# Layer attention with late scaling of its outputs, and norms split straight from PSUM

## The chip, the cores and the metric

The program runs on one core of one Trainium2 chip. The metric is the device time of one execution in microseconds (us). Two transformer blocks run one after the other in one launch.

## What is computed

The first block (attention over 8 grouped and 8 neighbourhood heads, a Fourier mix, a convolution, 16 experts) is followed by two layers of the second block; the change lies mostly in the layers.

```python
def hybrid_layer(x, ...):
    h = rms_norm_2(x, attn_norm_w)
    proj = h @ w_in
    mixed = concatenate([retention_mixer(...),   # 4 heads
                         dsa_mixer(...),         # 4 heads
                         dilated_mixer(...)])    # 8 heads
    x = x + mixed @ w_out
    h = rms_norm_2(x, mlp_norm_w)
    return x + jnp.square(jax.nn.relu(h @ w_up)) @ w_down

# dsa_mixer, per head, over the selected keys
p = jax.nn.softmax(jnp.where(valid, s, -jnp.inf), axis=-1)
return jnp.einsum('bhqn,bqnhd->bqhd', p, v_sel)
```

There are 512 tokens of width 1024, heads of 64 columns, and everything is float32. The three dilated branches come down to one softmax whose scores have the logarithm of a count added, so the 4 selected heads and the 8 dilated heads are the same computation, causal, with a different additive mask: 12 heads of "mixed attention" per layer.

## The kernel before

Every engine has one hand-written stream of instructions; semaphores tie them together (`T.next` works out the count to wait for), and loops are hardware loops. The order on each engine is the order in which the code is written.

Matrix products run as three float32r products of a rounded part and a remainder (`WH` and `WL` of a weight, `hH` and `hL` of an activation). A rounded part is made by ScalarE (ACT), the remainder by VectorE (DVE).

**Attention** (`attend` on TensorE (PE), ACT and DVE; `heads` on SyncE (SP), which issues the loads) works on tiles n of 128 query rows; a head has four (tt = 0 to 3), a pair of heads eight, and even and odd heads use buffers s = 0 and s = 1. In the layers tile tt sees (tt + 1) x 128 keys. For a tile, PE makes the scores (L816, L818); DVE adds the mask and takes the row's largest value in one instruction (L1838), then turns it into the exponential's bias (`NM`, L1752); ACT takes the exponential and sums it into `DEN` (L1278); DVE takes the reciprocal (L1759) and scales the probabilities with it (L1760); PE turns them (L828); ACT copies them out of PSUM (L1297). When a head's four tiles are there, PE multiplies with the values (L840) into `OT[s]`, 64 rows of bank 0. DVE then puts the head out (`put`, `to_split`, L2271 and L2272: the rounded part, then the remainder, each 64x512). In tile 1 of every head ACT rounds the next head's q and k (`rounded`, L1271, L1272), and DVE makes the remainders (`remainders`, L1737, L1738), after which PE may start that head's scores. DVE runs one tile ahead: in step n it issues

```python
top((n + 1) % (2 * NT), ...)
normalise(n)
...
if tt == 1:
    if not (last and s == 1):
        remainders(1 - s)
    ...put(i, 0) or put(i - 1, 1)
```

In the first pair of a layer, DVE also carries one piece of the norm of the retention heads per tile (`retention_norm`). SP loads the values of a head once that head has been put out (`head_oe`), and q and k of the pair after next behind it. The first block's two attentions use the same `attend`, with 768 keys per tile and with the gates' products and the convolution's taps beside it; the neighbourhood heads' mask is added in `na_bias`.

**A norm's split** (`turn` on PE, `split` on ACT and DVE): PE turns the normed activations, 128 columns k at a time, into one of two halves of `TP`; DVE scales them into SBUF (`F`, L1631); ACT rounds `F` into `hH` (L1175); DVE subtracts `hH` from `F` into `hL` (L1621). PE goes on to the next but one k when `F` has been written, and starts the product when all 8 have. A layer has two such norms, and a split of 2 columns k (the retention heads' output, L1629) ahead of the product with `w_out`.

## Time and profile before

| | |
|---|---|
| median of 3 runs | 3302.6 us (3300.22 to 3303.91) |
| profiled execution, its own time | 3302.91 us |
| its span | 3301.1 us |
| granted TensorE clock, mean over the span | 0.921 |
| busy: PE, DVE, ACT, POOL | 84%, 55%, 38%, 3% |
| mixed attention, layer 1 and layer 2 | about 1877 to 2011 us and 2717 to 2851 us of the span |

A span is counted from the first to the last recorded instruction; the execution's own time has 1.8 us more around it. Shares are means over stages whose limits differ: long stretches are products at a steady pace on PE, and the two mixed attentions are a tenth of the span in which four engines wait for each other. A row of the timeline gives start, duration, engine, line, operation, and in brackets how long the engine was idle before it and what ended that.

### The profile page before, as it was taken

How to read it: one execution, taken by the hardware profiler on the slowest of the kernel's cores; microseconds unless marked ns; L12 is line 12 of the kernel's file. 1: busy time of each engine (PE TensorE's matmuls, PEld its weight loads, DVE VectorE, ACT ScalarE, POOL GpSimd, SP SyncE). 2: the span in 40 equal slices, each digit the busy share in tenths (PEclk: the TensorE clock that was granted, in tenths of full speed). 3: DMA queues.
4: the chain of work that ended last, by engine and by line, in shares of the span. 5: the costliest groups of instructions: out<-in, count | busy, mean ns of one | idle time of the engine just before them, and what ended most of it. 6: DMA issues, size and time to landing. Idle time of an engine off the chain costs nothing. (4 is left out here: it accounts for less than half of the span.)

```text
span 3301.1 us, 34694 instructions
## 1 busy us (share of the span) xinstructions
PE 2773.3 (84%) x11775; PEld 2065.2 (63%) x11775; DVE 1830.0 (55%) x2919; ACT 1267.1 (38%) x1703; POOL 114.1 (3%) x172
## 2 busy tenths in 40 slices
PE   3889989888797599999399767899989976689998
PEld 0167566566576377777276545688868663468886
DVE  1145157577675688888537574444453657444444
ACT  1133246566413377777232242222233314332222
POOL 2001000000000100000001000000000100000000
PEclk9989999999998799999689888899988987889999
DMA  9656324344342599999224222222312332213232
GB/s 318 211 145 175 123 70 110 80 108 104 110 165 90 195 372 375 381 373 346 100 96 126 66 64 80 77 89 93 98 61 72 118 93 56 81 65 101 89 100 71
DMA packets 241586, 466.27 MB, mean 141 GB/s; under 512 B 67864, under 2 KB 90640, under 8 KB 241455
## 3 DMA queue, kind: packets, MB, share of 16 engines
q1 hardware_dynamic: 226383, 413.73, 38.4%
q0 software_dynamic: 15072, 50.87, 4.5%
q8 instruction: 73, 1.20, 0.2%
q14 instruction: 58, 0.48, 0.0%
HBM read 399.83 MB, written 64.72 MB: 141 GB/s over the span
## 5 line engine op out<-in xcount | busy, mean ns | idle before, releaser
L1574 DVE TENSOR_TENSOR WL<-W,WH 128x2048 fp32r<-128x2048 f32 x139 | 318.5, 2292 | 563.0 <-ACT WH L1116 557.2
L1116 ACT ACTIVATE WH<-W 128x2048 fp32r<-128x2048 f32 x139 | 265.7, 1912 | 735.8 <-PE BKP L689 643.9
L689 PE MATMUL BKP<-hH,WH 128*128 128x512 f32 x896 | 357.7, 399 | 24.8 <-DVE hL L1859 13.7
L689 PE MATMUL BKP<-hH,WL 128*128 128x512 f32 x896 | 353.6, 395 | 0.0
L689 PE MATMUL BKP<-hL,WH 128*128 128x512 f32 x896 | 353.4, 394 | 0.0
L689 PE MATMUL BKP<-WH,hH 128*128 128x512 f32 (+3 forms) x640 | 253.4, 396 | 30.1 <-DVE hL L1621 22.9
L689 PE MATMUL BKP<-WH,hL 128*128 128x512 f32 (+3 forms) x640 | 245.5, 384 | 0.0
L689 PE MATMUL BKP<-WL,hH 128*128 128x512 f32 (+3 forms) x640 | 244.9, 383 | 0.0
L689 PE MATMUL BKP<-WH,aH 128*128 128x512 f32 (+1 forms) x544 | 215.9, 397 | 22.5 <-DVE aL L2054 10.4
L689 PEld LDWEIGHTS BKP<-hH,WH 128*128 128x128 f32 x896 | 171.7, 192 | 68.1 <-issue 30.9
L689 PE MATMUL BKP<-WL,aH 128*128 128x512 f32 (+1 forms) x544 | 212.3, 390 | 0.0
L689 PE MATMUL BKP<-WH,aL 128*128 128x512 f32 (+1 forms) x544 | 211.9, 389 | 0.0
L689 PEld LDWEIGHTS BKP<-hL,WH 128*128 128x128 f32 x896 | 171.0, 191 | 36.6
L689 PEld LDWEIGHTS BKP<-hH,WL 128*128 128x128 f32 x896 | 171.7, 192 | 35.1
L1948 DVE TENSOR_TENSOR X<-X,BKP 128x512 f32<-128x512 f32 x144 | 97.3, 685 | 163.2 <-PE BKP L689 163.2
L828 PE MATMUL TPP<-IDN,AT 128*128 128x128 f32 x624 | 114.2, 310 | 83.4 <-DVE AT L1760 83.2
L689 PEld LDWEIGHTS BKP<-WH,hH 128*128 128x128 f32 x640 | 129.3, 202 | 68.6 <-issue 48.2
L828 PEld LDWEIGHTS TPP<-IDN,AT 128*128 128x128 f32 x624 | 80.8, 154 | 115.1 <-issue 93.9
L689 PEld LDWEIGHTS BKP<-WH,hL 128*128 128x128 f32 x640 | 129.2, 202 | 20.6
L689 PEld LDWEIGHTS BKP<-WL,hH 128*128 128x128 f32 x640 | 129.6, 203 | 18.8 <-issue 0.5
L689 PEld LDWEIGHTS BKP<-WH,aH 128*128 128x128 f32 x544 | 103.9, 191 | 54.1 <-DVE aL L2054 21.4
L709 PE MATMUL TPP<-IDN,BIG 128*128 128x128 f32 x208 | 47.0, 385 | 105.3 <-DVE BIG L1614 86.5
(365 smaller groups left out, 5466.0 us busy)
## 6 DMA issues: line engine op xcount, KB each, us to landing
W<-in_w_expert_gu_dram SPq DMA_DIRECT2D x46, 1024.0 KB, 8.4
G<-in_w_expert_gu_dram SPq DMA_DIRECT2D x46, 1024.0 KB, 8.5
W<-in_w_in_dram SPq DMA_DIRECT2D x42, 1024.0 KB, 5.7
W<-in_w_up_dram SPq DMA_DIRECT2D x32, 1024.0 KB, 5.4
W<-in_w_down_dram SPq DMA_DIRECT2D x32, 1024.0 KB, 5.0
W<-in_w_expert_down_dram SPq DMA_DIRECT2D x24, 1024.0 KB, 8.1
G<-in_w_expert_down_dram SPq DMA_DIRECT2D x22, 1024.0 KB, 8.3
X<-in_w_in_dram SPq DMA_DIRECT2D x16, 1024.0 KB, 8.5
```

The source lines that it names most:

```text
L689: mm = pe.matmul(BK[j][:, 0:cols], lt, rh, start=start and a == 0, stop=stop and a == len(q) - 1, skip_group_check=True)
L709: mm = pe.transpose(TP[:, c0:c0 + P], src(i, k), IDN[:])
L828: mm = pe.transpose(TP[:, bank + k0 - c0:bank + k0 - c0 + P], PR[n % 2][:, k0:k0 + P], IDN[:])
L1116: act.activation(WH[s][:], W[s][:], ACT.Copy).then_inc(sems["w_hi"], 1)
L1574: v.tensor_tensor(WL[s][:], W[s][:], WH[s][:].bitcast(F32), ALU.subtract).then_inc(sems["w_lo"], 1)
L1948: v.tensor_tensor(xs, xs, BK[j], ALU.add).then_inc(sems[BANKS[j]], 1)
```

## The change

In the layers' mixed attention, `attend` and `heads` are replaced by `mixed_attention` and `mixed_heads`. The probabilities are turned unscaled. DVE takes the reciprocal of `DEN` as an instruction with 64 equal columns into `RDW` (`inverse`, in `F`), and PE multiplies each such 128x64 tile with the identity, which gives the reciprocals as 64 rows of `RD2` (bank 1), beside the outputs in `OT2` (bank 0). Both heads of a pair are put out together, in tile 1 of the next pair: DVE copies `RD2` to SBUF (`YF`) and multiplies it with `OT2`, ACT rounds the result into `hH` (`output`, in tile 2), and DVE makes the remainder (`put_rest`, in tile 3). SP loads a head's values when PE has finished with the old ones (`head_o`) and no longer when DVE has put them out. The mask is added by one instruction that also multiplies by minus the scale and takes the smallest value, which is the exponential's bias itself: the instruction at L1752 is gone, here and in the first block, where without a mask the scale is folded into q. Where the layers split a norm, ACT and DVE both read the turned activations from PSUM and apply the scale themselves; `F` is not written, and PE goes on when the remainder is there.

```diff
-        PTB_2 = [(W[0][:],), (XN[:, :, 256:768],)]
+        PT2 = [W[0][:], XN[:, :, 256:768]]
+        SC2, OT2, RD2 = [SC[:, 0:512], BK[2]], BK[0], BK[1]
+        RDW = F[:, 1, :].rearrange("p (s t c) -> p s t c", s=2, t=NT)
+        YF = F[:, 0, :]
...
+                def later(i):
+                    for s in range(2):
+                        sp.wait_ge(sems["head_lo"], T.next("head_lo"))
+                        sp.sem_inc(sems["paused"], 1)
+                        qk(i * 2 + (6 + s), s)
+                    for s in range(2):
+                        sp.wait_ge(sems["head_o"], T.next("head_o"))
+                        sp.sem_inc(sems["paused"], 1)
+                        values(i * 2 + (6 + s), s)
+                T.loop(5, later)
...
-                heads(12, 4, S, before=after_retention)
+                mixed_heads()
...
+            def turn_direct(src, nk):
+                for k in range(nk):
+                    if k >= 2:
+                        pe.wait_ge(sems["norm_lo"], T.at("norm_lo", k - 1))
+                    for i in range(NT):
+                        c0 = (k % 2) * 512 + i * P
+                        mm = pe.transpose(TP[:, c0:c0 + P], src(i, k), IDN[:])
+                    mm.then_inc(sems["norm_tr"], 1)
...
+                def turned(n):
+                    pe.wait_ge(sems["head_exp"], T.next("head_exp"))
+                    pe.wait_ge(sems["head_ptc"], T.next("head_ptc:free"))
+                    for kt in range(n % NT + 1):
+                        c0 = n % 2 * 512 + kt * P
+                        mm = pe.transpose(TP[:, c0:c0 + P], PR[n % 2][:, kt * P:(kt + 1) * P], IDN[:])
+                    mm.then_inc(sems["head_pt"], 1)
+
+                def values(s, free=True):
+                    pe.wait_ge(sems["head_ptc"], T.next("head_ptc:full", NT))
+                    if s == 0 and free:
+                        pe.wait_ge(sems["head_y"], T.next("head_y"))
+                    pe.wait_ge(sems[f"head_landed{s}"], T.next(f"head_landed{s}", 16))
+                    rows = slice(s * HD, (s + 1) * HD)
+                    for kt in range(NT):
+                        pe.matmul(OT2[rows, kt * P:S], VS[s][:, kt, :], PT2[s][:, kt, kt * P:S], start=kt == 0,
+                                  stop=kt == NT - 1, skip_group_check=True)
+                    pe.wait_ge(sems["head_rd"], T.next("head_rd", NT))
+                    for tt in range(NT):
+                        mm = pe.matmul(RD2[rows, tt * P:(tt + 1) * P], RDW[:, s, tt, :], IDN[:], start=True, stop=True,
+                                       skip_group_check=True)
+                    mm.then_inc(sems["head_o"], 1)
+
+                def body(first, last):
+                    for n in range(2 * NT):
+                        if n + 2 < 2 * NT or not last:
+                            pe.wait_ge(sems["head_nm"], T.next("head_nm"))
+                            scores(n + 2)
+                        else:
+                            T.skip("head_nm")
+                        turned(n)
+                        if n % NT == 0 and not (first and n == 0):
+                            values(1 if n == 0 else 0, not first)
...
+            def split_direct(nk, dst, scale=None):
+                for k in range(nk):
+                    act.wait_ge(sems["norm_tr"], T.next("norm_tr"))
+                    src = TP[:, (k % 2) * 512:(k % 2) * 512 + S]
+                    if scale is None:
+                        ins = act.activation(dst[:, k, :], src, ACT.Copy)
+                    else:
+                        ins = act.activation(dst[:, k, :], src, ACT.Copy, scale=scale(k))
+                    ins.then_inc(sems["norm_hi"], 1)
...
-                    act.activation(QX[s], QS[s][:], ACT.Copy)
+                    act.activation(QX[s], QS[s][:], ACT.Copy, scale=1.0 if biased else SCALE)
...
+                def output(i):
+                    act.wait_ge(sems["head_y"], T.next("head_y"))
+                    act.activation(hH[:, bass.ds(i + 2, 1), :].rearrange("p a q -> p (a q)"), YF, ACT.Copy).then_inc(
+                        sems["head_yh"], 1)
+
+                def body(i, first, last):
+                    for n in range(2 * NT):
+                        s, tt = n // NT, n % NT
+                        if n + 1 < 2 * NT or not last:
+                            exponential((n + 1) % (2 * NT))
+                        if tt == 1 and not (last and s == 1):
+                            rounded(1 - s)
+                        if tt == 0:
+                            act.wait_ge(sems["head_o"], T.next("head_o:free"))
+                        act.wait_ge(sems["head_pt"], T.next("head_pt"))
+                        act.activation(PT2[s][:, 0:tt + 1, tt * P:(tt + 1) * P],
+                                       TP[:, n % 2 * 512:n % 2 * 512 + (tt + 1) * P].rearrange("p (k q) -> p k q", q=P),
+                                       ACT.Copy).then_inc(sems["head_ptc"], 1)
+                        if n == 2 and not first:
+                            output(i - 1)
...
+            def split_direct(nk, H, L, scale=None):
+                for k in range(nk):
+                    v.wait_ge(sems["norm_hi"], T.next("norm_hi"))
+                    src = TP[:, (k % 2) * 512:(k % 2) * 512 + S]
+                    if scale is None:
+                        ins = v.tensor_tensor(L[:, k, :], src, H[:, k, :].bitcast(F32), ALU.subtract)
+                    else:
+                        ins = v.scalar_tensor_tensor(L[:, k, :], src, scale(k), H[:, k, :].bitcast(F32), ALU.mult,
+                                                     ALU.subtract)
+                    ins.then_inc(sems["norm_lo"], 1)
...
-                        link(v.tensor_reduce(MX[:, c:c + 1], SCS[c][:, 0:nk], AX.X, ALU.max))
+                        ins = v.tensor_reduce(NM[:, c:c + 1], SCS[c][:, 0:nk], AX.X, ALU.max, negate=True)
                     else:
                         v.sem_inc(sems["paused"], 1)
-                        bias(n // NT, n % NT, SCS[c], SB[c], MX[:, c:c + 1])
-                    v.tensor_scalar(NM[:, c:c + 1], MX[:, c:c + 1], -SCALE, None, ALU.mult).then_inc(
-                        sems["head_nm"], 1)
+                        ins = bias(n // NT, n % NT, SCS[c], SB[c], NM[:, c:c + 1])
+                    ins.then_inc(sems["head_nm"], 1)
...
+                def top(n, bias):
+                    c, tt = n % 2, n % NT
+                    nk = (tt + 1) * P
+                    v.wait_ge(sems["head_s"], T.next("head_s"))
+                    v.sem_inc(sems["paused"], 1)
+                    v.tensor_tensor_reduce(SB[c][:, 0:nk], SC2[c][:, 0:nk], bias(tt), -SCALE, -TAKEN, ALU.add, ALU.min,
+                                           NM[:, c:c + 1]).then_inc(sems["head_nm"], 1)
+
+                def inverse(n):
+                    v.wait_ge(sems["head_exp"], T.next("head_exp"))
+                    v.reciprocal(RDW[:, n // NT, n % NT, :], DEN[:, n % 2:n % 2 + 1].to_broadcast([P, HD])).then_inc(
+                        sems["head_rd"], 1)
+
+                def put(i):
+                    v.wait_ge(sems["head_o"], T.next("head_o"))
+                    link(v.tensor_copy(YF, RD2))
+                    v.tensor_tensor(YF, OT2, YF, ALU.mult).then_inc(sems["head_y"], 1)
+
+                def put_rest(i):
+                    v.wait_ge(sems["head_yh"], T.next("head_yh"))
+                    part = lambda ap: ap[:, bass.ds(i + 2, 1), :].rearrange("p a q -> p (a q)")
+                    v.tensor_tensor(part(hL), YF, part(hH).bitcast(F32), ALU.subtract)
+
+                def body(i, first, last, bias, bias_next):
+                    for n in range(2 * NT):
+                        s, tt = n // NT, n % NT
+                        if n + 1 < 2 * NT or not last:
+                            top((n + 1) % (2 * NT), bias if n + 1 < 2 * NT else bias_next)
+                        if n == 0 and not first:
+                            v.wait_ge(sems["head_o"], T.next("head_o"))
+                        inverse(n)
+                        if first:
+                            beside(n)
+                        if tt == 1 and not (last and s == 1):
+                            remainders(1 - s)
+                        if n == 1 and not first:
+                            put(i - 1)
+                        if n == 3 and not first:
+                            put_rest(i - 1)
...
-                add_max(sb[:, 0:S], sc[:, 0:S], flat(ES[s][:, j0:j0 + 8, :]), MXC[:, 0:1])
-                link(add_max(sb[:, S:KEYS], sc[:, S:KEYS], RNW[:], MXC[:, 1:2]))
-                link(v.tensor_tensor(most, MXC[:, 0:1], MXC[:, 1:2], ALU.max))
+                c = tt % 2
+                add_min(sb[:, 0:S], sc[:, 0:S], flat(ES[s][:, j0:j0 + 8, :]), MXA[:, c:c + 1])
+                link(add_min(sb[:, S:KEYS], sc[:, S:KEYS], RNW[:], MXB[:, c:c + 1]))
+                return v.tensor_tensor(least, MXA[:, c:c + 1], MXB[:, c:c + 1], ALU.min)
...
-                split("norm", NK, hH[:], hL[:], lambda k: AF[:, 3, k:k + 1])
+                split_direct(NK, hH[:], hL[:], lambda k: AF[:, 3, k:k + 1])
...
-                def to_split(k0):
-
-                    def go(i, s):
-                        part = lambda ap: ap[s * HD:(s + 1) * HD, bass.ds(i + k0, 1), :].rearrange("p a q -> p (a q)")
-                        link(v.tensor_copy(part(hH), OT[s]))
-                        v.tensor_tensor(part(hL), OT[s], part(hH).bitcast(F32), ALU.subtract).then_inc(sems["head_oe"], 1)
-                    return go
```

On DVE, in a steady pair of heads, from the mask of tile 2 to the mask of tile 3 (`QS` and `KS` are q and k of the head to come, `W`/`AT` the masked scores, `BKP`/`SCP` PSUM). Before:

```order
L1838 ISA AT,MX<-SCP,ES 128x384 [waits head_s]
L1838 ISA MX 128x1
L1752 TENSOR_SCALAR NM<-MX 128x1 [waits dve_self]
L1759 RECIPROCAL RD<-DEN 128x1 [waits head_exp]
L1760 TENSOR_SCALAR AT<-AT,RD 128x256 [waits dve_self]
...
L1737 TENSOR_TENSOR WH<-QS,WH 64x512 [waits head_hi]
L1738 TENSOR_TENSOR WH<-KS,WH 128x512
...
L2271 COPY hH<-BKP 64x512
...
L2272 TENSOR_TENSOR hL<-BKP,hH 64x512
...
L1838 ISA W,MX<-BKP,ES 128x512 [waits head_s]
```

In the change, with the pair before put out at this place:

```order
L2019 ISA AT,NM<-SCP,ES 128x384 [waits head_s]
L2019 ISA NM 128x1
L2024 RECIPROCAL F<-DEN 128x64 [waits head_exp]
...
L2010 TENSOR_TENSOR WH<-QS,WH 64x512 [waits head_hi]
L2011 TENSOR_TENSOR WH<-KS,WH 128x512
...
L2029 COPY F<-BKP 128x512 [waits head_o]
...
L2030 TENSOR_TENSOR F<-BKP,F 128x512 [waits dve_self]
...
L2019 ISA W,NM<-BKP,ES 128x512 [waits head_s]
```

Two instructions of each tile are gone (L1752, L1760), the reciprocal is 64 wide, and putting out is two instructions of 128 rows for every second head.

On PE, around the product with the values of an even head. Before:

```order
L828 MATMUL TPP<-IDN,AT 128x128 [waits head_ptc]
...
L840 MATMUL BKP<-W,VS 64x512 [waits head_landed0]
L840 MATMUL BKP<-W,VS 64x384
L840 MATMUL BKP<-W,VS 64x256
L840 MATMUL BKP<-W,VS 64x128
```

In the change:

```order
L942 ISA [waits head_y]
L945 MATMUL BKP<-W,VS 64x512 [waits head_landed0]
L945 MATMUL BKP<-W,VS 64x384
L945 MATMUL BKP<-W,VS 64x256
L945 MATMUL BKP<-W,VS 64x128
L947 ISA
L949 MATMUL BKP<-IDN,F 64x128 [waits head_rd]
L949 MATMUL BKP<-IDN,F 64x128 x3
```

Four matmuls of 128 columns follow the values of every head, and the even head's wait for `head_y` is one that DVE gives once a pair.

## Rows read from the trace of the kernel before

**Rows 1.** Busy us by engine and stretch of layer 1's mixed attention; PEclk is 0.63, 0.85

```profile
1877.00:1904.00 27.00, 14.34 (x44) 8.22 (x44) 23.02 (x69) 11.75 (x30) 0.00 (x0) 0.63 0.21 58
...
1920.00:2000.00 80.00, 55.82 (x215) 33.48 (x214) 56.81 (x193) 39.90 (x111) 0.00 (x0) 0.85 0.21 56
```

The columns are the stretch, its length, the busy time of PE, of PE's weight loads, of DVE, ACT and POOL (each with its count of instructions), the granted clock, the DMA engines' share and GB/s.

**Rows 2.** Waits, 1920 to 2003 us: waiter, waited for, total, times, longest

```profile
PE TPP L828 <- DVE AT L1760: 23.2, 14, 2.7
...
DVE WH L1737 <- ACT WH L1272: 11.2, 8, 1.8
```

**Rows 3.** Timeline of ACT and DVE, one head, and the remainders five heads later

```profile
1937.88 0.61 ACT L1278 ACTIVATE AT<-AT,NM 128x384 f32<-128x384 f32 x1 [0.32 <-DVE NM L1752]
...
1939.66 0.69 DVE L1737 TENSOR_TENSOR WH<-QS,WH 64x512 fp32r<-64x512 f32 x1 [1.35 <-ACT WH L1272]
...
1940.97 0.68 DVE L2271 CAST hH<-BKP 64x512 f32 x1
...
1942.38 0.67 DVE L1838 CUSTOM_DVE_ANT_0 W<-BKP,ES 128x512 f32<-128x512 f32 x1
...
1943.10 0.15 DVE L1752 TENSOR_SCALAR NM<-MX 128x1 f32<-128x1 f32 x1
...
1943.29 0.72 ACT L1278 ACTIVATE AT<-W,NM 128x512 f32<-128x512 f32 x1 [2.44 <-DVE NM L1752]
...
1943.69 0.28 DVE L1838 CUSTOM_DVE_ANT_0 AT<-SCP,ES 128x128 f32<-128x128 f32 x1
...
1944.88 0.49 ACT L1297 ACTIVATE BIG<-TPP 128x384 f32<-128x384 f32 x1 [0.78 <-PE TPP L828]
...
1946.16 0.60 ACT L1297 ACTIVATE BIG<-TPP 128x512 f32<-128x512 f32 x1 [0.41 <-PE TPP L828]
...
1989.36 0.69 DVE L1737 TENSOR_TENSOR WH<-QS,WH 64x512 fp32r<-64x512 f32 x1 [1.36 <-ACT WH L1272]
```

**Rows 4.** The reciprocals by width (ns), and a copy 64 wide (total us, mean ns)

```profile
L1759 DVE RECIPROCAL RD<-DEN x48: 152/154/165, 1880.6 to 2003.0; 128x1 f32<-128x1 f32 x48
L2007 DVE RECIPROCAL SM<-SM x1: 178/178/178, 1090.9 to 1090.9; 128x4 f32<-128x4 f32 x1
L2199 DVE COPY BIG<-TPP 128x64 f32<-128x64 f32 x32 | 6.8, 222 | 19.6 <-PE TPP L1055 19.0
```

**Rows 5.** Timeline of PE, the products with the values at either clock

```profile
1937.19 2.36 PE L840 MATMUL BKP<-W,VS 128*64 128x512 f32 x8
...
2005.34 4.03 PE L840 MATMUL BKP<-BIG,VS 128*64 128x512 f32 x8 [0.87 <-ACT BIG L1297]
```

**Rows 6.** Timeline of DVE and SP, the end of layer 1's mixed attention

```profile
2009.40 0.69 DVE L2271 CAST hH<-BKP 64x512 fp32r<-64x512 f32 x1 [5.72 <-PE BKP L840]
...
2011.15 16.14 SPq L298 DMA_DIRECT2D W<-in_w_out_dram  x4
```

**Rows 7.** Timeline, the split of the retention heads' columns

```profile
2020.58 1.29 DVE L1629 COPY F<-TPP 128x512 f32<-128x512 f32 x2
...
2023.50 0.76 PE L689 MATMUL BKP<-WH,hH 128*128 128x512 f32 x1 [11.40 <-DVE hL L1621]
```

**Rows 8.** Timeline, a layer's first norm split, to its first product

```profile
1620.97 3.93 PE L709 MATMUL TPP<-IDN,BIG 128*128 128x128 f32 x16 [49.38 <-DVE BIG L1614]
1622.13 1.60 DVE L1631 TENSOR_SCALAR F<-TPP,AF 128x512 f32<-128x512 f32 x2 [1.21 <-PE TPP L709]
1622.91 0.63 ACT L1175 ACTIVATE hH<-F 128x512 fp32r<-128x512 f32 x1 [7.31 <-DVE F L1631]
...
1623.65 0.68 DVE L1621 TENSOR_TENSOR hL<-F,hH 128x512 fp32r<-128x512 f32 x1
...
1632.80 0.79 PE L689 MATMUL BKP<-hH,WH 128*128 128x512 f32 x1 [2.30 <-DVE F L1631]
```

**Rows 9.** Waits of the first block's attentions, 446 to 655 and 655 to 880 us

```profile
ACT AT L1278 <- DVE NM L1752: 35.4, 16, 4.3
...
ACT AT L1278 <- DVE NM L1752: 51.2, 18, 6.0
```

124 lines of the change are left out of this document (100 added, 24 removed).

## Prediction

> **What bounds the kernel now.** I read the waits of the mixed attention first, then one head in the timeline, then the spots around it where everything stands still.
>
> In the steady stretch of the mixed attention (80 us, eight heads) no engine is full: DVE is busy 56.8 us, PE 55.8, ACT 39.9 [rows 1]. So the limit is a chain that goes from engine to engine. Its pitch is (1989.36 - 1939.66) / 5 = 9.94 us a head [rows 3]; I use 9.9. The chain is in the same rows. The exponential of tile 2 starts at 1937.88; behind it ACT rounds the next head's q and k, and DVE can start the remainders at 1939.66, after 1.35 us of idling. They take 1.31 us, putting out the head before takes 1.41 (1940.97 to 1942.38), and then only does DVE come to the mask of tile 3, whose exponential starts at 1943.29, after ACT has stood idle for 2.44 us. PE meanwhile waits for probabilities that DVE is still to scale: 23.2 us in 83 [rows 2]. In the first 27 us, with the retention norm beside it, DVE itself is the bound (23.0 of 27 busy) and PE's granted clock is 0.63, mostly the lower level [rows 1].
>
> The norms' splits and the mixed attention's end are pure latency: the products with the weights wait for them.
>
> **The change, step by step.**
>
> *Wide reciprocal.* The trace has none. A reciprocal takes 154 ns at width 1 and 178 at width 4, 8 ns an element, so 0.154 + 63 x 0.008 = 0.66 us at width 64; a copy 64 wide takes 0.22 [rows 4]. These are the ends. I take 0.66, since its rows are of the same operation, but it rests on a single 128x4 row. The Trainium skill (VectorE: DVE Perf Modes, section on the 8-slice pipeline in each mode) says that a reciprocal is an iterative divide with a repeat count of 8; the slope of 8 ns, where a copy's is about 1, agrees. The Trainium skill (Vector Engine (DVE) Microarchitecture Reference, section 3.2 on a single slice) speaks of one chain that spans all eight slices, which read as a pipeline would give the short price; that case is a rival below.
>
> *A head of the steady stretch.* From one tile-2 exponential to the next, with the durations of [rows 3], in the change:
> - The head in which the pair is put out: rounding 1.78, remainders 1.31, copy and product 1.41 (two 512-wide instructions, as now). Mask of tile 3 and its exponential: 0.91 before, less 0.11 for the instruction that is gone, 0.80: ACT starts it at 5.30. Then on ACT the exponential 0.75, the copy of tile 2 0.49, the new rounding of the outputs 0.60 (a 128x512 copy from PSUM): 7.14. DVE makes the remainder (0.70 with the signal): 7.84. Mask of tile 1 0.43, reciprocal 0.66, mask of tile 2 0.56, signals 0.13: 9.6 us.
> - The other head has no putting out: 1.78 + 1.31 + 0.80 = 3.89 to the exponential of tile 3, 0.85 to its sum, then on DVE reciprocal 0.70, mask 0.47, reciprocal 0.70, mask 0.56 and 0.08: 7.3 us.
>
> A pair takes 16.9 us where it takes 19.8, and four pairs a layer: -11.6, say -11. PE has room for its new work only at the higher clock. Its values take 2.36 us there for 1280 columns [rows 5]; 512 more columns cost 0.4 of that, 0.94, and they end 2.5 us after the exponential of tile 2, ahead of DVE, which wants them at 3.1. At the lower clock (4.03) they would cost 1.6.
>
> *The first pair,* bound by DVE. Bias, reciprocal and scaling take 0.59 us a tile of 384 (1943.10 to 1943.69) [rows 3], some 0.6 in the mean, against 0.70: +0.8 for 8 tiles; one putting out moves to the next pair, -1.4. Sum -0.6. For the second pair, at the lower clock, I take 0: earlier turns against 1.6 us of added products.
>
> *The end.* The last tile's reciprocal and scaling (0.76) go from between exponential and PE. The last products gain 1.6 at the lower clock. SP's load of `w_out` no longer waits for putting out (1.41 of the 1.75 between 2009.40 and 2011.15) [rows 6]; that now lies beside the load. Sum -0.6.
>
> *Two-column split.* DVE's two copies (1.29) go, and ACT rounds beside DVE's weight remainder: 2023.50 comes 1.4 earlier [rows 7].
>
> A layer: -11 - 0.6 - 0.6 - 1.4 = -13.6; both: -27.
>
> *Norm splits,* four. From the first turn to the first product 11.83 us: eight times DVE's two instructions, 1.46 a column block, and a start and an end [rows 8]. Now a half of `TP` goes round PE (1.16), ACT (0.74), DVE (0.68, and 0.13 for the signal) in 2.71 us, for two blocks; four turns take 0.98 (3.93 / 4). The eighth block's turns start at 0.98 + 3 x 2.71 = 9.1 and the product at 10.1, since nothing waits behind them: -1.7 each, -7. DVE's remainder now reads PSUM; as a 512-wide instruction it stays under 0.8 and is not the limit.
>
> *The first block.* The bias instruction goes; it lies 0.19 us ahead of an exponential (1943.10 to 1943.29) [rows 3], and 34 of 64 exponentials waited for it [rows 9]: at most -6.5. PE is the fuller engine there and gets part of it back. Against that the remainder of q becomes an instruction with a factor, under +0.1 us for each of 16 heads. I take -3, between +1.5 and -6.5. Folding the scale, swapping largest for smallest and the second set of small tiles cost nothing, as the instructions keep their widths; were that wrong by 0.1 us a tile, the 64 tiles would give back 6.
>
> Sum: -27 - 7 - 3 = -37 us. Against the profiled execution's own time of 3302.9, which is 0.3 above the median of the runs, that is 3266. I forecast 3265.
>
> **The rivals.**
>
> *Cheap wide reciprocal (0.22 us).* For it: the output of a reciprocal has one element a column like a copy's. Against: the slope between the two widths. The put-out head falls by 0.44 to 9.2, the other to 6.9, where ACT takes over: pair 16.1, four pairs -15; the first pair -0.6 - 8 x 0.44 = -4.1. A layer -21, both -42: 3250.
>
> *The clock in one head of each pair.* The products with the values of one head run at the lower level, 4.03 + 1.6 us, and keep DVE waiting for `head_o`, or for the next scores, 1.9 us longer (5.0 in place of 3.1). Then a pair takes 18.8: four pairs -4, with the rest of a layer about -1: -10 in both. 3283. For it: the mean clock of the steady stretch is 0.85 and not 1, so a part of it runs at the lower level already [rows 1].
>
> *Slower: the clock in every head.* PE's added products come behind the values, and in the first 27 us, where PE was busy for only 14.3, its clock was 0.63 [rows 1]. With both heads at the lower level a pair costs 16.9 + 3.8 = 20.7, and scores and turns at half speed add about 1, against 19.8: +1.9 a pair, +7.6 a layer, +3 in the first pairs. With -2 at the end, +17 in both layers, and -7 and -3 elsewhere: 3310. It decides from the point where the values and the four added products take over 3.1 + 0.9 us. Against it: PE is asked to do more in less time, and its share of busy time in the steady stretch, 0.70, would rise.
>
> **How the numbers follow.** Forecast 0.48, cheap reciprocal 0.22, one slow head 0.18, all slow 0.12. About 0.2%, 6.6 us, is what a measurement of this kernel tells from no change. Faster: 0.48 + 0.22 + nearly all of the 0.18, less something for a first block or a wait that I priced wrongly, 0.85; the slow case spreads over slower 0.10 and the same 0.05. The range for 8 in 10 goes from the cheap reciprocal with the first block's best (3250 - 6, and a little for the second pair) to past one slow head: 3241 to 3294.
>
> **What would show it.** In the changed kernel's trace: 96 reciprocals 128x64 at 0.66 us or at 0.22; a pitch of alternately 9.6 and 7.3 us between remainders; the four added products taking 0.94 us behind the values, and a granted clock of 0.85 or more in the steady stretch; no wait of DVE for bank 0 or 1; the first product of a norm 10.1 us after its first turn; `w_out`'s load issued within 0.4 us of PE's end. It is wrong if DVE waits for PE before putting out, if the loads of q and k, which now start when `head_o` comes, hold up ACT's rounding, or if the clock stays at its lower level.

## The result, and the profile after

The changed kernel takes 3253.17 us in the median (3252.39 to 3257.71, 4 runs), where the kernel before took 3302.16 (4 runs) beside it: a ratio of 0.9852, 95% interval 0.984 to 0.9863, 49 us less. The forecast was 3265, between 3241 and 3294. Its profiled execution took 3253.63 us, with a span of 3251.7.

The steady stretch of the mixed attention (layer 1), as in [rows 1]: the busy time of PE, of its weight loads, of DVE, ACT and POOL, the granted clock, the DMA engines' share, GB/s.

```profile
1923.00:1987.00 64.00, 52.96 (x262) 32.50 (x262) 45.44 (x120) 39.91 (x113) 0.00 (x0) 0.95 0.23 64
```

These 64 us hold 7.6 heads (eight took 67.6), the 80 us before held eight. DVE spends 45.4 us on them, 6.0 a head, where it spent 56.8, or 7.1 a head; ACT, which now rounds the outputs too, spends the same 39.9. PE, at 0.70 before, is now busy for 0.83 of the time, and its clock is 0.95 where it was 0.85. Head by head (from one head's first remainder to the next; the same columns):

```profile
1908.85:1917.68 8.83, 6.76 (x27) 3.53 (x26) 6.83 (x17) 5.47 (x15) 0.00 (x0) 0.79 0.47 135
1917.68:1927.57 9.89, 9.16 (x42) 5.97 (x41) 5.17 (x15) 4.96 (x14) 0.00 (x0) 0.84 0.06 15
1927.57:1936.57 9.00, 6.84 (x40) 4.48 (x39) 6.83 (x18) 5.48 (x15) 0.00 (x0) 1.00 0.48 131
1936.57:1943.36 6.79, 6.09 (x32) 3.70 (x31) 5.08 (x14) 4.96 (x14) 0.00 (x0) 1.00 0.08 19
1943.36:1952.35 8.99, 6.92 (x41) 4.57 (x39) 6.84 (x17) 5.47 (x15) 0.00 (x0) 1.00 0.46 131
1952.35:1959.15 6.80, 6.11 (x32) 3.71 (x31) 5.10 (x14) 4.95 (x14) 0.00 (x0) 1.00 0.09 19
1959.15:1968.12 8.97, 6.90 (x31) 3.91 (x30) 6.83 (x17) 5.47 (x15) 0.00 (x0) 0.84 0.46 132
1968.12:1976.40 8.28, 7.33 (x39) 4.69 (x38) 5.12 (x14) 4.83 (x14) 0.00 (x0) 0.97 0.07 16
```

The first, third, fifth and seventh are heads in which a pair is put out; they take 8.8 to 9.0 us whatever the clock. The other head takes 6.8 where the clock stayed at 1.00 in the put-out head ahead of it, and 8.3 to 9.9 where it had fallen there. A pair thus takes 15.8 at its best, where it took 19.9 [rows 3]. The timeline of DVE and ACT in the put-out head, to set beside [rows 3]:

```profile
1930.20 0.68 DVE L2019 CUSTOM_DVE_ANT_0 W<-BKP,ES 128x512 f32<-128x512 f32 x1
1930.81 0.08 DVE L2019 DVE_READ_ACCUMULATOR2_ANT NM<- 128x1 f32 x1
1930.81 0.55 DVE L2024 RECIPROCAL F<-DEN 128x64 f32<-128x64 f32 x1
1930.93 0.72 ACT L1434 ACTIVATE AT<-W,NM 128x512 f32<-128x512 f32 x1 [1.22 <-DVE NM L2019]
...
1931.28 0.23 DVE L2019 CUSTOM_DVE_ANT_0 AT<-SCP,ES 128x128 f32<-128x128 f32 x1
```

The wide reciprocal is an instruction of 0.55 us, and the next one starts 0.47 after it. The steps at the attention's end and the norm's split, as in [rows 6 to 8]: DVE's putting out, SP's load of `w_out` and the first product with it; then the first turn of layer 1's norm, its second pair of column blocks and the first product.

```profile
1994.86 0.69 DVE L2029 COPY F<-BKP 128x512 f32<-128x512 f32 x1 [4.16 <-PE BKP L949]
1995.14 10.57 SPq L301 DMA_DIRECT2D W<-in_w_out_dram  x3
...
2006.26 0.76 PE L723 MATMUL BKP<-WH,hH 128*128 128x512 f32 x1 [8.05 <-DVE hL L1802]
```

```profile
1624.84 1.97 PE L753 MATMUL TPP<-IDN,BIG 128*128 128x128 f32 x8 [49.55 <-DVE BIG L1771]
...
1627.52 1.97 PE L753 MATMUL TPP<-IDN,BIG 128*128 128x128 f32 x8 [0.71 <-DVE hL L1804]
...
1634.50 0.78 PE L723 MATMUL BKP<-hH,WH 128*128 128x512 f32 x1
```

From the start of the last putting out to the first product it is 11.4 us (14.1 before), from a norm's first turn to its first product 9.66 (11.83), and the turns come round every 2.68 us.

**Where the time went,** from the two timelines. I cut an execution into three: the first block's attention (ACT's first exponential to the first turn of the norm behind it), the stretch of the experts (from there to layer 1's first turn, which the change does not touch), and the layers.

| us | before | changed |
|---|---|---|
| first block's attention | 611.5 | 608.0 |
| stretch of the experts | 561.9 | 568.6 |
| layers, to the end | 1680.1 | 1626.9 |

The layers give 53 us and the first block 3; the expert stretch, the same code, took 6.7 longer in this execution. Whether that is the change's doing is one of the questions below. These are single executions: in a second one of each kernel the layers took 1677.3 and 1628.4, so their gain is 49 to 53.

### The profile page after: what moved, and what is told of

The parts are those of the page before. It is cut to its first block and busy times, and to the rows that moved or that the text cites. A ratio compares the mean times of both kernels' runs of the same rounds, so it can differ in the third digit from the quotient of the medians.

```text
span 3251.7 us, 34520 instructions
## 1 busy us (share of the span) xinstructions
PE 2771.0 (85%) x11967; PEld 2075.6 (64%) x11967; DVE 1771.0 (54%) x2615; ACT 1270.8 (39%) x1715; POOL 114.3 (4%) x172
## 3 DMA queue, kind: packets, MB, share of 16 engines
q8 instruction: 75, 1.23, 0.2%
## 5 line engine op out<-in xcount | busy, mean ns | idle before, releaser
L1731 DVE TENSOR_TENSOR WL<-W,WH 128x2048 fp32r<-128x2048 f32 x139 | 318.6, 2293 | 549.9 <-ACT WH L1218 544.1
L723 PE MATMUL BKP<-WH,aH 128*128 128x512 f32 (+1 forms) x544 | 215.1, 395 | 23.1 <-DVE aL L2286 10.5
L723 PEld LDWEIGHTS BKP<-WL,hH 128*128 128x128 f32 x640 | 130.4, 204 | 18.4 <-issue 0.5
L1063 PE MATMUL BKP<-WH,hH 128*128 128x512 f32 x276 | 113.7, 412 | 14.0 <-DVE WL L2306 10.8
L2306 DVE TENSOR_TENSOR WL<-W,WH 128x2048 fp32r<-128x2048 f32 x46 | 105.4, 2291 | 25.4 <-ACT WH L1541 25.2
L2306 DVE TENSOR_TENSOR WL<-G,WH 128x2048 fp32r<-128x2048 f32 x45 | 103.0, 2290 | 28.4 <-ACT WH L1541 28.4
```

The source lines that it names most:

```text
L723: mm = pe.matmul(BK[j][:, 0:cols], lt, rh, start=start and a == 0, stop=stop and a == len(q) - 1, skip_group_check=True)
L1063: pe.matmul(dst, ah[:, k0 + kk, :], wh[:, kk, c], start=k0 + kk == 0, stop=False, skip_group_check=True)
L1731: v.tensor_tensor(WL[s][:], W[s][:], WH[s][:].bitcast(F32), ALU.subtract).then_inc(sems["w_lo"], 1)
L2306: v.tensor_tensor(ring_l(m, s0), ring_w(m, s0), ring_h(m, s0).bitcast(F32), ALU.subtract).then_inc(sems["w_lo"], 1)
```

## The experiments

The theory at this point: the mixed attention is still a chain over the engines; the change took DVE's work out of it, and what remains of the pair is set by putting out in one head, and in the other by PE's order at whichever clock it has. The rivals: the gain comes from elsewhere (norms, first block); the price of the reciprocal decides; PE's clock and room decide, not its order. Every ratio is to the kernel before, run on the same chip. Medians of different chips are not compared more closely than their ratios; for small differences I use the three stretches, one execution each.

**The two kernels again.**

> The changed kernel itself, unaltered, beside the others. Of its steady pairs two patterns were seen in profiled executions: the put-out head always takes 9.0 us; the other takes 6.8 where TensorE's granted clock stayed at 1.00 through the put-out head, and 8.0 to 9.9 where a part of that head had the lower level. Theory (which pattern holds is a matter of the single execution, and sets most of its spread): 3253 in the median, lowest and highest some 6 to 10 apart. Rival (the pattern is set by the kernel): within 3 of each other.

Measured: 3251.08 us (3249.14 to 3266.19), ratio 0.9871, interval 0.985 to 0.9891. Both patterns are there: in layer 1 the other head took 7.0 and 6.8 us in the first two steady pairs, then 8.5 and 8.3; in layer 2 all pairs were slow, where in the first execution two of the four other heads of layer 2 took 6.8 and 6.7. One slow pair:

```profile
2730.33:2739.32 8.99, 6.96 (x30) 3.85 (x29) 6.84 (x18) 5.47 (x15) 0.00 (x0) 0.81 0.45 131
2739.32:2747.39 8.07, 7.25 (x40) 4.71 (x39) 5.12 (x14) 4.95 (x14) 0.00 (x0) 1.00 0.07 16
```

So the pattern is a matter of the single execution, as the theory had it, and changes from pair to pair within one; the spread of 17 us was wider than forecast, by one run at 3266. The timeline of the slow pair shows how the clock in one head costs time in the next (PE and DVE):

```profile
2733.72 0.38 PE L926 MATMUL BKP<-WH 128*128 128x256 f32 x1 [1.14 <-DVE NM L2019]
...
2736.58 3.63 PE L945 MATMUL BKP<-W,VS 128*64 128x512 f32 x8 [0.15 <-issue]
2740.05 1.04 PE L949 MATMUL BKP<-IDN,F 128*64 128x128 f32 x8
2741.01 0.50 PE L926 MATMUL BKP<-WH 128*128 128x512 f32 x1
...
2741.94 0.69 DVE L2019 CUSTOM_DVE_ANT_0 W<-BKP,ES 128x512 f32<-128x512 f32 x1 [1.23 <-PE BKP L927]
```

The values take 3.63 us in place of 2.36, since the granted clock (the column after POOL's) had fallen to the lower level:

```profile
2733.00:2736.00 3.00, 1.55 (x9) 1.04 (x9) 2.25 (x8) 2.31 (x7) 0.00 (x0) 0.96 0.52 153
2736.00:2737.50 1.50, 1.34 (x3) 0.43 (x4) 1.50 (x7) 1.03 (x4) 0.00 (x0) 0.50 0.57 178
2737.50:2739.32 1.82, 1.82 (x4) 0.67 (x3) 0.47 (x2) 1.75 (x4) 0.00 (x0) 0.54 0.56 178
2739.32:2741.00 1.68, 1.68 (x13) 1.28 (x11) 1.38 (x2) 0.00 (x0) 0.00 (x0) 1.00 0.00 0
```

Ahead of the fall PE was busy for only half of three us, since it waited for DVE's mask. That does not tell a slow pair from a fast one, though: the same three us of a pair of the first execution whose clock did not fall look alike.

```profile
1930.23:1933.23 3.00, 1.55 (x9) 1.03 (x9) 2.24 (x8) 2.30 (x7) 0.00 (x0) 1.00 0.54 148
```

Why the clock falls in one pair and not in the next stays open; what the runs show is its price. Behind the values in PE's one order stand the four added products and the scores of tile 3, and for these DVE waits 1.23 us.

> The kernel before itself, unaltered, to see a second profiled execution of it. From the first turn of the norm behind the first block to the first turn of the first layer (the expert stretch, which the change doesn't touch) its first one took 561.9 us; in nine executions of other kernels of this study it took 561.9 to 569.7. Theory (variation of single executions): a ratio of 1 within 0.002, and a stretch anywhere between 560 and 570. Rival (the changed kernel gives some 4 us back there): again under 563.

Measured: 3302.98 us (3293.21 to 3307.75, 12 runs), ratio 1.0, interval 0.999 to 1.0009. The stretch of the experts took 565.3 us, the first block 611.0, the layers 1677.3. Over the fourteen executions that I have, the expert stretch runs from 561.9 to 569.7 with no order by kernel (561.9 and 565.3 for the kernel before, 568.6 and 561.9 for the changed one). The theory holds, and the rival's "under 563" did not come: no give-back has to be assumed, though one of 2 or 3 us could not be seen.

**Parts of the change.**

> The kernel before, with only the six splits of the layers (four norms, two of two columns) made straight from PSUM; attention and the first block as before. In the changed kernel a layer's first product comes 9.66 us after the first turn where it came 11.83 us after it, and the two-column split ends 1.2 to 1.4 us earlier. Theory (this is a part of the gain that stands by itself): 4 x 2.2 + 2 x 1.3 = 11 us less, 3291. The sum of the prediction had 7 + 2.8 = 10 less. Rival (what follows the split waits for something else, the weights' conversion for one, and catches up): 0 to 4 less, 3298 to 3302.

```diff
-                turn("norm", cols_of(XN), NT, NK)
+                turn_direct(cols_of(XN), NK)
...
-                split("norm", NK, hH[:], hL[:], lambda k: AF[:, 3, k:k + 1])
+                split_direct(NK, hH[:], hL[:], lambda k: AF[:, 3, k:k + 1])
```

Measured: 3291.36 us, ratio 0.9961, interval 0.9946 to 0.9976 (-13 us, -8 to -18); the layers took 1667.3, 11 less than the mean of the two executions of before (1678.7). The theory holds; nothing behind the splits caught up.

> The changed kernel with the first block's attention as before: the largest score found with its sign, one instruction 128x1 for the bias of the exponential, the scale in the exponential. Mixed attention and splits stay as changed. Theory (the first block gave the forecast 3 us, and the 6.6 us that the expert stretch took longer in the profiled execution of the changed kernel are the variation of single executions): 3253 + 3 = 3256. Rival (the expert stretch is longer because of the first block's change, whose stores and loads come at other times): the two cancel or more, 3247 to 3252.

```diff
-                        ins = v.tensor_reduce(NM[:, c:c + 1], SCS[c][:, 0:nk], AX.X, ALU.max, negate=True)
+                        link(v.tensor_reduce(MX[:, c:c + 1], SCS[c][:, 0:nk], AX.X, ALU.max))
...
+                    v.tensor_scalar(NM[:, c:c + 1], MX[:, c:c + 1], -SCALE, None, ALU.mult).then_inc(
+                        sems["head_nm"], 1)
```

Measured: 3252.89 us, ratio 0.984, interval 0.9827 to 0.9853. By the time alone that decides nothing: it lies inside the spread of the changed kernel. The stretches decide it. The first block's attention took 610.6 us here, and 610.7 to 611.5 in the three other executions with the old code; with the new code it took 607.6 to 609.6 in ten executions. That is 2.6 us less, near the forecast's 3. The rival (a longer expert stretch by the first block's change) falls: it took 565.9 here, in the middle of all.

> The changed kernel with each head put out by itself (copy, product, ACT's rounding and DVE's remainder of 64 rows, for every head, behind the next head's remainders), as the kernel before did it; outputs scaled as changed. Theory (a 512-wide instruction costs the same for 64 rows as for 128, and putting out lies on the chain of its head): both heads take 9.0, a pair 18.0 in place of 15.8 to 17.05, so +1 to +2.2 in each of 8 steady pairs, and +2 a layer in the first two pairs, 12 to 22 more than the changed kernel: 3264 to 3274. Rival (the other head has slack, since TensorE's order holds it): 0 to 4 more, 3252 to 3256, and pairing was worth nothing.

```diff
-                    link(v.tensor_copy(YF, RD2))
-                    v.tensor_tensor(YF, OT2, YF, ALU.mult).then_inc(sems["head_y"], 1)
+                    link(v.tensor_copy(YF[r, :], RD2[r, :]))
+                    v.tensor_tensor(YF[r, :], OT2[r, :], YF[r, :], ALU.mult).then_inc(sems["head_y"], 1)
...
                         if n == 1 and not first:
-                            put(i - 1)
+                            put(i - 1, 1)
+                        if n == 5:
+                            put(i, 0)
```

Measured: 3276.3 us (3274.62 to 3279.8), ratio 0.9921, interval 0.9908 to 0.9934; layers 1653.6. Two steady heads:

```profile
1928.97:1938.46 9.49, 7.50 (x31) 4.15 (x30) 7.11 (x17) 5.69 (x15) 0.00 (x0) 0.82 0.44 124
1938.46:1947.48 9.02, 7.42 (x43) 4.93 (x42) 6.86 (x18) 5.47 (x15) 0.00 (x0) 1.00 0.06 15
```

The rival (slack in the other head) falls: both heads are long, 18.4 to 19.5 a pair. The layers took 26 us more than the changed kernel's, in the slowest of unpaired's five executions; by the ratios it is 17 (beside a_again) to 23 us more, where the theory had 12 to 22. The first of each two heads takes 9.5 and not 9.0. In that head rows 64 to 127 are put out: the copy, the product and the mask of tile 3 start 0.72, 0.73 and 0.73 us after the instruction ahead of each on DVE, where with rows 0 to 63 it is 0.61, 0.71 and 0.61. That is 0.25 of the 0.5; the rest comes at ACT's rounding and behind it. Together with b_norms this divides the layers' gain: 11 us for the splits, 1667 - 1654 = 14 for scaling outputs (with the bias instruction that went), 1654 - 1628 = 26 for putting out in pairs, of which 17 to 23 are left by the ratios. In either reckoning the last is the largest.

**The price of the wide reciprocal.**

> The changed kernel with a copy 128x64 in the place of each wide reciprocal (the division by the sum is left out). The price should go from 0.55 to 0.22 us in 96 instructions. Theory (a chain in the steady pairs, DVE in the first pair): one wide instruction lies on the chain of the put-out head, none on that of the other head, where ACT is full: -0.33 in each of 5 pairs, 8 x -0.33 in the first pair, about -4.5 a layer, 3244. Rival 1 (each lies on the chain): 96 x 0.33 = 32 less, 3221. Rival 2 (DVE has room, ACT and PE set the pitch): 3253, and the forecast's dear reciprocal would have cost nothing against the cheap one.

```diff
-                    v.reciprocal(RDW[:, n // NT, n % NT, :], DEN[:, n % 2:n % 2 + 1].to_broadcast([P, HD])).then_inc(
+                    v.tensor_copy(RDW[:, n // NT, n % NT, :], DEN[:, n % 2:n % 2 + 1].to_broadcast([P, HD])).then_inc(
```

> The changed kernel with a reciprocal of 128x1 and the spreading left to TensorE: the stationary operand of the added products reads the one column with a stride of 0, 64 times. Output as in the changed kernel. The reciprocal costs 0.154 in place of 0.55. Theory: as with the copy and a little more, 3242. Rival (reading the weights with a stride of 0 slows the load of weights, or the shorter wait moves nothing): 3253 or more.

```diff
-                    v.reciprocal(RDW[:, n // NT, n % NT, :], DEN[:, n % 2:n % 2 + 1].to_broadcast([P, HD])).then_inc(
+                    v.reciprocal(RDN[:, n:n + 1], DEN[:, n % 2:n % 2 + 1]).then_inc(
...
-                        mm = pe.matmul(RD2[rows, tt * P:(tt + 1) * P], RDW[:, s, tt, :], IDN[:], start=True, stop=True,
+                        mm = pe.matmul(RD2[rows, tt * P:(tt + 1) * P], RDN[:, s * NT + tt:s * NT + tt + 1].to_broadcast([P, HD]), IDN[:], start=True, stop=True,
```

Measured: 3247.54 us, ratio 0.983 (0.9817 to 0.9843) with the copy; 3248.34, ratio 0.9826 (0.9813 to 0.9839) with the narrow one. The prices of the three, from the lines' own view (shortest, median and longest ns) of the changed kernel, r_copy and r_narrow:

```profile
L2024 DVE RECIPROCAL F<-DEN x96: 546/548/554, 1883.8 to 2802.2; 128x64 f32<-128x64 f32 x96
```

```profile
L2024 DVE COPY F<-DEN x96: 187/191/197, 1878.0 to 2793.6; 128x64 f32<-128x64 f32 x96
```

```profile
L2024 DVE RECIPROCAL F<-DEN x96: 155/159/165, 1879.2 to 2796.7; 128x1 f32<-128x1 f32 x96
```

The theory had 3244 and 3242, 4 and 6 us too low. Rival 1 (32 us) falls: the layers took 1622.8 and 1625.3, 2 to 6 us less than the changed kernel's 1626.9 and 1628.4. Of r_narrow's rival one half falls with the price of the weight loads, shown at the end of this document; the other half, that the shorter wait moves nothing, holds for the steady pairs. The gain is where DVE is the bound: from the first to the fourth head's remainder 28.23 us became 26.09 and 25.86. In the steady pairs the copy gave nothing where the clock stayed at 1.00:

```profile
1917.51:1926.26 8.75, 6.69 (x38) 4.33 (x37) 5.59 (x18) 5.36 (x15) 0.00 (x0) 1.00 0.47 131
1926.26:1933.29 7.03, 6.32 (x34) 3.94 (x33) 3.80 (x14) 4.96 (x14) 0.00 (x0) 1.00 0.09 23
```

8.75 + 7.03 = 15.78 against 8.99 + 6.80 = 15.79: what the put-out head wins, the other loses, waiting for PE. So the theory's -0.33 for each steady pair was wrong too. That a ring through PE's products holds the pair is my reading of it; the next run tests it.

**TensorE: room or order?**

> The changed kernel with the four added products of every head made twice (the second time over the same rows), 1.04 us more of TensorE a head at the higher clock. Theory (they stand on the path of the other head, ahead of the scores of tile 3; in the put-out head DVE waits for them after 0.5 us of slack): +1.0 and +0.5 a pair, 1.5 x 10 = 15 more, 3268. Rival (a fuller TensorE keeps its clock at the higher level and wins back what it costs): 3250 to 3256. Rival of the forecast's accounting (the added products lie beside other work, in the put-out head and in the other): 3253.

```diff
-                    for tt in range(NT):
+                    for tt in [*range(NT), *range(NT)]:
                         mm = pe.matmul(RD2[rows, tt * P:(tt + 1) * P], RDW[:, s, tt, :], IDN[:], start=True, stop=True,
```

Measured: 3255.01 us (3247.65 to 3260.26), ratio 0.986 (0.9842 to 0.9877); layers 1635.9, 8 us more than the changed kernel. This profile is of the slowest of its four executions; the median is only 4 us above that of a_again on the same chip, where the theory had 15. The theory and the rival of the fuller TensorE are both right in part:

```profile
1925.80:1935.34 9.54, 7.79 (x49) 5.44 (x47) 6.93 (x17) 5.47 (x15) 0.00 (x0) 1.00 0.43 115
1935.34:1943.01 7.67, 6.86 (x40) 4.55 (x39) 5.14 (x15) 4.95 (x14) 0.00 (x0) 1.00 0.10 28
```

The pitches rise by 0.5 and 0.9, as the theory had it, so the added products do stand on the path of both heads. But the clock stays at 1.00 in all steady pairs but the first of layer 1, and 17.2 us a pair is hardly more than the 17.06 of the changed kernel's slow pattern. It is not this one execution alone: the mean clock over the whole program was 0.931 to 0.934 in its four executions, and 0.926 to 0.929 in the nine of the changed kernel.

> The changed kernel with DVE's putting out (two instructions, 1.37 us) moved from ahead of the mask of tile 3 to behind its reciprocal, ACT's rounding and DVE's remainder of it one tile later each. Theory (in the put-out head the chain goes through putting out to the mask of tile 3): the exponential of tile 3 comes 1.37 earlier, the mask of the next tile then waits for the putting out, so of it 0.5 to 1.3 a pair remain: 5 to 13 less in ten pairs, 3240 to 3248. Rival (TensorE, whose work is in one order with the values in it, holds the pair): no change, 3253; and were putting out in the way of the next tile as much as of this one, also none.

```diff
-                        if n == 1 and not first:
+                        if n == 2 and not first:
                             put(i - 1)
```

Measured: 3244.71 us (3236.2 to 3246.69), ratio 0.983 (0.9814 to 0.9846), layers 1623.1: 4 to 5 us less in these, 6 by the median beside a_again, within the theory's range. But it is not the steady pairs that give it:

```profile
1928.80:1936.66 7.86, 7.06 (x39) 4.60 (x38) 5.15 (x14) 4.96 (x14) 0.00 (x0) 0.99 0.07 17
1936.66:1945.78 9.12, 7.81 (x33) 4.24 (x32) 6.84 (x18) 5.46 (x15) 0.00 (x0) 0.83 0.45 129
```

The put-out head is not shorter (9.1), the other not much (7.9 for 8.07 in the slow pattern). What the exponential of tile 3 wins, the next head's mask loses, and PE's order still stands behind. The 4 us lie at the end of each layer's attention. From the last remainders to the last putting out it takes 16.5 us with the last values at the higher clock (2.37 us) and 18.1 at the lower (3.97 us), where the changed kernel had 18.5 and 20.1: 2 us a layer at either. The theory's mechanism was therefore not borne out, and that its number was is luck.

> As put_late, and TensorE's products with the values (with the four added ones behind them) come one tile later, behind the scores and turns of tile 3 and 1 instead of ahead of them. Theory (the other head is held by TensorE's order: values 2.36 and added products 1.04 stand ahead of the scores of tile 3, at the lower clock 4.0 and 1.6; that makes its pitch 6.8 or 8 to 10): the pitch of the other head becomes the same at either clock, about 6.8. The excess over 6.8 in the profiled execution of the changed kernel is 3.1 + 1.5 + 1.5 + 2.9 = 9 us in its eight steady heads of this kind, so 9 less than put_late, 3232 to 3240. Rival (TensorE's room is what counts and not its order): the same as put_late.

```diff
-                        if n % NT == 0 and not (first and n == 0):
-                            values(1 if n == 0 else 0, not first)
+                        if n % NT == 1 and not (first and n == 1):
+                            values(1 if n == 1 else 0, not first)
```

Measured: 3233.92 us (3230.49 to 3240.38), ratio 0.9805 (0.979 to 0.982); layers 1613.0, 10 less than put_late.

```profile
1933.56:1940.32 6.76, 5.71 (x32) 3.57 (x31) 5.05 (x14) 4.83 (x15) 0.00 (x0) 1.00 0.18 49
1940.32:1949.08 8.76, 7.54 (x40) 4.62 (x39) 6.75 (x18) 5.47 (x16) 0.00 (x0) 1.00 0.39 113
```

All of the other heads in both layers take 6.6 to 6.8 now, as the theory had it, and the rival falls: the same matmuls in another order give it. At the higher clock alone a pair is 15.5 for 15.8. Over both layers the other heads give 8.2 us, since none is slow any more, the put-out heads 2.0, and the stretch from the last remainders to the last putting out 5.5 (14.6 us in each layer for 16.5 and 18.1); the head ahead of the steady stretch takes 3.4 back. Whether that is because the mask no longer waits behind slow values or because the clock no longer falls can't be told apart here, since it did not fall in the steady pairs. At the higher clock the other head was 6.8 in the changed kernel already, so there PE's order was not what held it: in the steady pairs the order costs time only with a fallen clock. The one head ahead of the steady stretch got longer (10.5 us for 8.8), as DVE's putting out now waits there for the added products (0.96 us of it).

**A faster order.**

> As late_two, and DVE makes the remainders of the next head's q and k behind the mask of tile 3 instead of ahead of it. In late_two DVE idles for 1.35 us ahead of them, waiting for ACT's rounding, while the scores of tile 3 lie ready, and ACT idles for 1.8 us for that mask. Theory (the mask of 0.7 us falls into that idle time and ACT runs on): 0.7 a head of 20 steady ones, 14 less, 3220. Rival (the scores of the next head's first tile wait for the remainders and take the mask's place on the chain, or TensorE loses its clock): 3230 to 3238.

```diff
+                        if tt == 2 and not (last and s == 1):
+                            remainders(1 - s)
                         inverse(n)
                         if first:
                             beside(n)
-                        if tt == 1 and not (last and s == 1):
-                            remainders(1 - s)
```

> late_three with the reciprocal of 128x1 and the spreading left to TensorE's weights of stride 0. Theory (with the order of TensorE and DVE mended, DVE is the fuller engine of a pair, some 12 of 15 us, so that the 0.4 us of each of 96 instructions counts in the first pair, 2.4 a layer as seen with r_narrow, and for a part in the steady ones): 5 to 20 less than late_three. Rival (as with r_narrow, only the first pair gains): 5 less. Rival 2 (TensorE idles more, and its clock falls): no less than late_three.

Measured: late_three 3229.82 us, ratio 0.9777 (0.9764 to 0.979), layers 1605.9; with the narrow reciprocal 3220.96 (3220.34 to 3226.38), ratio 0.9757 (0.9743 to 0.977), layers 1601.9. This last one computes all that the changed kernel does and beats both, by 81 us and, by the ratios, some 31 to 38. Its steady pair, below, is 14.8 us. late_three itself gave half of what the theory had (7 in the layers for 14): the other head fell from 6.76 to 5.97, and the put-out head rose by 0.2, with PE busy for 8.0 of its 8.95 us.

```profile
1913.86:1922.72 8.86, 7.91 (x45) 5.12 (x44) 5.45 (x17) 5.46 (x16) 0.00 (x0) 1.00 0.38 109
1922.72:1928.68 5.96, 4.91 (x27) 2.96 (x26) 3.80 (x15) 4.62 (x15) 0.00 (x0) 1.00 0.20 58
```

The narrow reciprocal again gains in the first pair alone (28.6 to 25.6 us over three heads, in each layer), as the rival had it with 5 us. The layers as a whole took 4 us less. The medians say 9, which is in the theory's range, but of the 9.4 us between the two profiled spans 5.4 lie ahead of the layers, where the two kernels are alike.

## Why the prediction was right, and where it was not

What the forecast said would bring the gain did: no engine is full, and taking DVE's scaling, the bias instruction and every second putting out from between the engines shortened every steady pair. The size was too small by a quarter (-37 for -49), and nearly every term erred to that side. The measured 3253 lies nearer to the rival of the cheap reciprocal, 3250, than to the 3265 of the forecast; that is chance, since the reciprocal was not cheap. The path within a pair was not as drawn, either. The forecast led the put-out head through putting out to the mask of tile 3, and in put_late putting out was moved off that path and the head stayed at 9.1. It led the other head through two wide reciprocals on DVE, and in r_copy both became 0.36 us cheaper and the head went from 6.80 to 7.03. What exactly holds each head is not fully shown; PE's added products lie on the path of both (rd_double), which the forecast had beside it.

- *Wide reciprocal:* forecast 0.66 us, measured 0.549, (549 - 154) / 63 = 6.3 ns an element and not 8. It was taken from one row of width 4. The Trainium skill's repeat count of 8 (VectorE: DVE Perf Modes, the 8-slice pipeline) speaks for a price of several times a copy's, and 549 ns against 191 for a copy of the same width and operand agrees with that in kind, if not in the factor. The cheap price (0.22) did not come true, and its worth had been set wrongly as well: with 0.19 us in place of 0.55 only the first pairs gained, 4 to 6 us of layers in all.
- *A steady pair:* forecast 9.6 + 7.3 = 16.9, measured 9.0 + 6.8 = 15.8 at the higher clock. The forecast had added durations, where the starts lie closer together. From DVE's remainder of the outputs to the next exponential of tile 2 it added 0.70 + 0.43 + 0.66 + 0.56 + 0.13 = 2.48 us; in the timeline it is 1.95:

```profile
1932.83 0.69 DVE L2035 TENSOR_TENSOR hL<-F,hH 128x512 f32 x1 [0.50 <-ACT hH L1439]
1933.44 0.42 DVE L2019 CUSTOM_DVE_ANT_0 W<-BKP,ES 128x256 f32<-128x256 f32 x1
...
1933.78 0.55 DVE L2024 RECIPROCAL F<-DEN 128x64 f32<-128x64 f32 x1
...
1934.24 0.50 DVE L2019 CUSTOM_DVE_ANT_0 AT<-SCP,ES 128x384 f32<-128x384 f32 x1
...
1934.78 0.61 ACT L1434 ACTIVATE AT<-AT,NM 128x384 f32<-128x384 f32 x1
```

  Over the second to the last pair the forecast had 0 for the second, -11 for four, and of the end -0.76 + 1.6: -10 in all. Measured from the fourth head's remainders to the last putting out of layer 1 were 86.0 us for 100.0 before (layer 2: 85.8 for 99.8), so -14. In the second executions of both kernels it was 87.1 for 99.8 and 88.3 for 98.2, so -13 and -10: the forecast is at the edge of what the clock's patterns spread.
- *The second rival, the clock in one head of each pair,* came true in a part of the pairs. Of the two places that it named, `head_o` and the next scores, it was the second: DVE's wait for the scores of tile 3 in the other head, which stand behind the values and the added products in PE's order. It costs 1.3 to 3.1 us where it happens. I gave it 1.9 for all pairs or none; that it comes and goes within one layer was not foreseen. The third rival (slower than before) did not show: PE's mean clock rose from 0.85 to 0.95.
- *The first pair:* forecast -0.6, measured 32.21 - 28.23 = -4.0 over three heads. This is the single term that failed by most, 3.4 us a layer: 0.59 us for a tile of 384, "some 0.6 in the mean, against 0.70: +0.8 for 8 tiles". From the row of the accumulator to the start of what follows, a tile of 384 took 0.72 us in the first pair before (0.68 in the mean of the four widths); now it is 0.47 at any width, since the reciprocal starts with the accumulator's read and ends beside its successor. Before, then in the changed kernel:

```profile
1887.11 0.08 DVE L1838 DVE_READ_ACCUMULATOR2_ANT MX<- 128x1 f32 x1
...
1887.83 1.22 DVE L2212 TENSOR_TENSOR G<-BIG 128x1024 f32<-128x1024 f32 x1
```

```profile
1890.09 0.55 DVE L2024 RECIPROCAL F<-DEN 128x64 f32<-128x64 f32 x1
1890.56 1.16 DVE L2444 TENSOR_TENSOR G<-BIG 128x1024 f32<-128x1024 f32 x1
```

  DVE wins some 0.2 a tile where I had it lose 0.1. The forecast had begun to count at the bias instruction, 0.12 us behind the accumulator's row, and had charged the reciprocal its whole duration and more. The 10 tiles between the first and the fourth remainders give -2.1, and the putting out that moved on gives its -1.4.
- *The end and the two-column split:* forecast -0.6 and -1.4. From the last putting out to the first product it is 14.1 - 11.4 = -2.7: of it 1.75 - 0.28 = 1.5 up to SP's load, as forecast, and 1.2 behind it for 1.4. The forecast had then offset the first by the added products at the lower clock, +1.6. In the first execution the last values and added products came at the higher one (2.37 and 1.04 us); in a_again they came mostly at the lower (3.62 and 1.50, 3.77 and 1.36) and the last putting out 1.5 us later, so that term, too, depends on the execution.
- *Norm splits:* forecast -1.7 each, measured 11.83 - 9.66 = -2.2; period 2.68 for 2.71. b_norms gives 11 in the layers for 10 of norms and two-column splits.
- *First block:* forecast -3, measured -2.6. The remainder of q with a factor cost nothing (690 ns for 689 before).
- *Sum:* -37 forecast; -49 to -53 in the layers and -2.6 in the first block, with up to 8 us of variation in the expert stretch; -49 by the medians, and -43 by the ratio of a_again.

## What to carry to other kernels

Where no engine is full, look not only at which wait ends last but at what stands in the waiting engine's order ahead of the instruction that is wanted: here the same matmuls, one tile later, were worth 10 us. What is narrow in rows costs as much as what is wide (0.68 us for 64x512 on DVE, 0.69 for 128x512), so joining two heads' 64 rows into 128 was the largest single part (17 to 26 us). And a chain is priced from start to start, in the old and in the new alike: durations overlap, and sums of them overstated what the steady pair and the first pair would take.

## What the runs showed of the hardware

- A reciprocal of 128x64 on DVE takes 549 ns, of 128x1 154 to 159, a copy of 128x64 from a column with stride 0 191 ns.
- TensorE loads weights from one column with a stride of 0 as fast as from 64 columns. The lines' view of r_narrow, beside 136/137/232 in the changed kernel:

```profile
L949 PEld LDWEIGHTS BKP<-IDN,F x192: 137/137/231, 1890.1 to 2802.7; 128*64 128x64 f32 x192
```

- A wide reciprocal's successor on DVE starts 0.47 us after it, before its 0.55 us are over.
- On DVE, instructions of the putting out on rows 64 to 127, and the one behind them, start 0.72 to 0.73 us after the one ahead, those on rows 0 to 63 after 0.61 to 0.71 (unpaired).
- The same program ran with two patterns of TensorE's clock in its steady pairs, 15.8 us long or mostly 17.06, also within one execution. With the added products made twice the clock stayed at 1.00 in seven of eight steady pairs, at 1.4 us more a pair than the fast pattern. A part of what work costs on TensorE can come back through its clock.
